# Spreading the last projections over twelve heads, and mixing tile 0 one head later

## The reference, cut to what matters

```python
proj = einsum('bsd,de->bse', rmsnorm(x), w_in)      # a_u a_v a_z b_q b_k b_v b_z i_q i_k i_w
ya = spatial_gating(a_u, a_v, ...)                  # branch A
yb = sparse_attention(q, k, b_v, qi, ki, wi)        # branch B: 8 heads, 256 keys of each row
oa, ob = rmsnorm(ya per group), rmsnorm(yb per head)
mixed = concat([oa * silu(a_z), ob * silu(b_z)])
x = x + einsum('bse,ed->bsd', mixed, w_out)
```

## Time and profile before

| | |
|---|---|
| runs | 601.02, 600.10, 600.96 us; median 600.96 us |
| span of the profiled execution, first to last instruction | 597.3 us |
| PE busy | 561.4 us (94%) |
| DVE busy | 448.7 us (75%) |
| ACT busy | 375.5 us (63%) |
| POOL busy | 229.4 us (38%) |
| mean granted PE clock | 0.983 of full |

### The profile page before, as it was taken

One profiled execution on the slowest core, in us unless ns is written; L12 is line 12 of the kernel. 1 busy time (PEld: TensorE's weight loads), 2 busy tenths in 40 slices (PEclk: granted clock), 3 DMA queues, 4 the chain that ended last, 5 costly groups with the idle time before them and its releaser, 6 DMA issues.

```text
span 597.3 us, 9151 instructions
## 1 busy us (share of the span) xinstructions
PE 561.4 (94%) x3038; PEld 477.2 (80%) x3038; DVE 448.7 (75%) x1142; ACT 375.5 (63%) x743; POOL 229.4 (38%) x300
## 2 busy tenths in 40 slices
PE   8798999989999999979999997999989899999987
PEld 7796888868878888868878786888878788898866
DVE  4574788889999887778999557788777877657631
ACT  6573767757898885757877645655455455555510
POOL 5686432118865456675333425731011010102020
PEclk9899999989999999999999997899999999999999
DMA  8622210012321112212112337012201102020122
GB/s 238 223 72 62 63 36 18 2 36 73 105 88 38 53 37 54 71 36 54 35 54 88 98 120 224 0 54 72 81 26 49 58 10 62 19 72 2 36 71 70
DMA packets 39982, 39.69 MB, mean 66 GB/s; under 512 B 6144, under 2 KB 28160, under 8 KB 39936
## 3 DMA queue, kind: packets, MB, share of 16 engines
q1 hardware_dynamic: 38896, 39.11, 22.1%
q10 hardware_dynamic: 1040, 0.00, 0.1%
HBM read 30.72 MB, written 8.39 MB: 65 GB/s over the span
## 4 chain that ended last, share of the span: by engine, by line
PE 52%; DVE 25%; POOL 10%; issue 6%; ACT 4%; DMA 2%; DVEq 0%; SPq 0%; POOLq 0%; ACTq 0%
PE ps_proj L1071 15%; PE ps_proj L1237 11%; PE ps_proj L1207 5%; PE ps_lg L1099 4%; PE ps_lg L1098 4%; PE ps_tp L1192 4%; DVE y_a L1577 3%; DVE rank L1456 2%; POOL w_lo L620 2%; PE ps_lg L1237 2%; DVE eq L1456 2%; DVE cand L1467 2%; DVE delta L1472 2%; POOL stage L615 2%; POOL y_a L682 1%
## 5 line engine op out<-in xcount | busy, mean ns | idle before, releaser
L1071 PE MATMUL ps_proj<-w_hi,xT_hi 128*128 128x512 f32 (+1 forms) x432 | 166.4, 385 | 5.6 <-POOL w_lo L620 4.3
L1071 PE MATMUL ps_proj<-w_lo,xT_hi 128*128 128x512 f32 (+1 forms) x432 | 162.5, 376 | 0.0
L1071 PE MATMUL ps_proj<-w_hi,xT_lo 128*128 128x512 f32 (+1 forms) x432 | 162.4, 376 | 0.0
L908 ACT ACTIVATE ps_lg<-score,cand 128x768 f32<-128x768 f32 (+2 forms) x96 | 96.2, 1002 | 27.5 <-DVE cand L1467 27.5
L620 POOL TENSOR_TENSOR w_lo<-stage,w_hi 128x512 fp32r<-128x512 f32 x48 | 64.5, 1344 | 97.1 <-ACT w_hi L769 97.1
L1071 PEld LDWEIGHTS ps_proj<-w_hi,xT_hi 128*128 128x128 f32 x432 | 82.8, 192 | 19.9 <-POOL w_lo L620 5.6
L1071 PEld LDWEIGHTS ps_proj<-w_lo,xT_hi 128*128 128x128 f32 x432 | 82.5, 191 | 15.1
L1071 PEld LDWEIGHTS ps_proj<-w_hi,xT_lo 128*128 128x128 f32 x432 | 83.0, 192 | 12.4
L973 ACT CAST xT_hi<-ps_tp 128x512 fp32r<-128x512 f32 (+3 forms) x96 | 43.9, 483 | 63.8 <-PE ps_tp L1192 63.5
L1699 DVE TENSOR_TENSOR xT_lo<-ps_tp,xT_hi 128x512 fp32r<-128x512 f32 (+3 forms) x96 | 50.8, 553 | 33.7 <-ACT xT_hi L973 33.3
L732 POOL TENSOR_TENSOR yz<-hi_f,lo_f 128x512 f32<-128x512 f32 x8 | 10.3, 1285 | 124.7 <-DVE hi_f L1716 124.0
(11 more groups left out here) (176 smaller groups left out, 1169.2 us busy)
## 6 DMA issues: line engine op xcount, KB each, us to landing
stage<-in_w_in_dram SPq DMA_DIRECT2D x48, 256.0 KB, 2.6
x_in<-in_x_dram SPq DMA_DIRECT2D x8, 512.0 KB, 6.0
lo_f<-in_x_dram SPq DMA_DIRECT2D x7, 512.0 KB, 4.0
out_dram<-lo_f SPq DMA_DIRECT2D x7, 512.0 KB, 3.5
q_scratch<-nat SPq DMA_DIRECT2D x8, 256.0 KB, 2.1
q_in<-q_scratch SPq DMA_DIRECT2D x8, 256.0 KB, 3.3
stage<-in_w_out_dram SPq DMA_DIRECT2D x8, 256.0 KB, 2.7
z_scratch<-nat SPq DMA_DIRECT2D x8, 256.0 KB, 2.0
```

The costliest lines, as they stand in the source:

```text
L908: act.activation(ps_lg[i % 2][:, 0:keys(t)], score[:, sc_off[t]:sc_off[t] + keys(t)], ACT.Sign, bias=cand[:, t:t + 1].bitcast(F32), scale= ...
L1071: mm = pe.matmul(ps_proj[u % 2][:, 0:n], a[:, k, rows], b[:, k, 0:n], start=(k == 0 and i == 0), stop=(k == KB - 1 and i == 2))
```

## The change

The 32 blocks are allotted 2, 2, 2, 2 to heads 0 to 3 and 3 each to heads 4 to 11, where they were 3 each for heads 0 to 9 and 2 for head 10. Everything that is worked out from the list moves with it: units 4 to 7 are now completed in heads 3, 6, 9 and 11 (tanh, gate, store and the cast of a w_out block go with them), and `W_FROM` is 12. And DVE's `mix_b(0)` stands at the end of head 13 in place of head 12; the later tiles' stay where they were.

```diff
-        STEPS_BZ = [3] * 10 + [2]
+        STEPS_BZ = [2] * 4 + [3] * 8
...
                     if h == 2 and t > 0:
                         y_sums(t - 1)
-                    if h == 4 and t > 0:
+                    if h == (5 if t == 1 else 4) and t > 0:
                         mix_b(t - 1)
```

## The result

The changed kernel takes 603.95 us (median of 20 runs, 601.16 to 606.86), the kernel before 600.14 us (20 runs, 597.21 to 603.29): ratio 1.0059, 95% interval 1.0044 to 1.0073. It is slower by 0.6%: 3.5 us by the ratio, 3.8 by the two medians. That is outside the range of the prediction (600.0 to 603.2), on the side that it held a little less likely than no change.

A forecast was written before the change was run, and what follows sets the result against it. Between 362.7 and 377.2 the chain from unit 7 to the mix, not PE's speed, was taken to set the end. Terms of -0.04 up to 377.15 and +1.3 for the clock, on 600.96, gave 602.2 us; range 600.0 to 603.2.

The forecast's parts named there:

- W_out's second half: Casts, splits and scales of w_out's second half come a head later, first needed in head 17, hidden: costed at nothing.
- Heads 0 to 10 and unit 7: Head 0 saves nothing, the 0.22 us wait goes, head 10 ends about 1.65 us earlier; unit 7 complete 1.37 us later.
- Heads 11 to 13: Head 11's 2.67 us wait is filled; PE waits some 1.85 us for `lo_pT(11)`, replacing both old waits.
- The chain to the mix: From unit 7, durations stay: store 2.92 us, factors 1.37 us later, `mix_b(0)` 1.67 us, ending at 374.46.
- rival B: Chain from unit 7: store lands in 2.0 us or `mix_b` takes 0.7; time 600.3, down to 600.0; chance 0.12.
- The place of the mix: `mix_b(0)` in head 13 lets `mT(0, 0)` run at about 369.2, before the wait; first output block 377.15 against 377.19.
- The clock: After a wait of nearly 5 us PE stays at 1.2 GHz until 380.0, losing 1.3 us from the first output block.
- Rival C: Heads 11 to 13 at full clock: less low clock is itself a gain, 1.8 us, time 599.2; chance 0.08.

The follow-up runs named there:

- the two freed runs: Changed kernel with tile 0's mixing on POOL freed of unit 7: 597.57 us (0.9948); also with tile 1's mixing before the last split: 597.78 us (0.9938).

## Why the prediction was wrong

**The step that failed** is "W_out's second half": "Casts, splits and scales come a head later. They are first needed in head 17 ... I cost these at nothing." It asked when PE needs the blocks, and that part is right: no profile shows PE waiting for a block of this half in heads 17 to 22. It did not ask what stands behind the last split on POOL. `finish_b(1)` does, and DVE needs it in head 20. The price of the late casts, by the marks, is 24.1 - 21.6 = 2.5 us where the prediction had nothing: 1.5 for `finish_b(1)` behind the last split, 1.0 for POOL's scale and split falling beside DVE's steps. By the medians the casts alone cost 1.9 us, and taking tile 1's mixing out of that place, or the casts back, removed some 2.8 of the change's 3.5 us. All rivals of the prediction lay before head 15; none had this mechanism.

**Heads 0 to 10 and unit 7** were right. Head 0 saved nothing (a wait of 0.53), the 0.22 us wait went, and unit 7 was complete at 363.34 (its blocks in the chain start at 361.27 and take 2.07), which is 363.86 with the 0.52 added, where 364.04 was worked out.

**Heads 11 to 13** were right: 1.72 us before `pv(5)`, where 1.85 was worked out; `mT(0, 0)` at 368.55 + 0.52 = 369.07, worked out 369.2.

**The chain to the mix** was right in kind, and a little long. The mix began at 371.48 and took 1.66 us, so `mT(0, 1)` ran at 373.19 + 0.52 = 373.71, worked out 374.55. In this execution the store was not the last thing that `yz` waited for:

```profile
367.78 1.28 POOL L732 TENSOR_TENSOR yz<-hi_f,lo_f 128x512 f32<-128x512 f32 x1
```

It has no wait at all: POOL was itself busy till then, with the split and two scales, and the gap of 0.73 us that lay there before was not needed. In this execution rival B all but came true up to head 15: `mT(0, 1)` before 373.8, the first output block at 376.55, where it had 376.4 or earlier. The second profile of the changed kernel (the change again; first scores at 332.20, so 0.64 us is to be taken off) goes as forecast. Its `yz` waits for the store, and `mT(0, 1)` comes at 374.85 - 0.64 = 374.21 after a wait of 4.51:

```profile
369.43 1.28 POOL L732 TENSOR_TENSOR yz<-hi_f,lo_f 128x512 f32<-128x512 f32 x1 [0.47 <-DMA z_scratch<-nat]
...
374.85 1.12 PE L1230 MATMUL ps_tp<-ident,hi_f 128*128 128x128 f32 x4 [4.51 <-DVE hi_f L1724]
```

Its first output block is at 377.68 - 0.64 = 377.04, worked out 377.15. The loss of the change stands behind this point in both. (One reading of the prediction was wrong without effect: not all of PE's waits in rows 3 end with DVE; the one of 2.67 us ends with ACT.)

**The place of the mix** was right in mechanism, as the run without the move shows (4.72 and 6.16 us of waiting), with 0.7 us in the medians, not beyond doubt.

**The clock.** Forecast was 1.2 GHz till 380.0, a loss of 1.3 us. The profiled execution had full clock back at about 376.4; the second one of the same kernel, entered 1.16 us later, at about 379.8 (PE: stretch and its length, busy, granted clock, DMA):

```profile
376.00:376.50 0.50, 0.50 (x3) 0.56 0.00 0
```

```profile
379.50:380.00 0.50, 0.50 (x3) 0.71 0.00 0
```

From the first output block to the return of the clock are 0.4 and 2.1 us. At the prediction's own rate that is a loss of 0.2 us in the first and 1.0 in the second, whose middle stretch is 24.9 in place of 24.1. So the term varies from one execution to the next, and 1.3 was above both. What nearness the forecast time has to the measured one, 602.2 to 603.95, is luck: a loss that was smaller than forecast stood for one that I had not seen, and the sum started from the 600.96 us of three runs, where twenty gave 600.14.

**Rival C,** that less low clock is a gain as such, fell for the change: the first profile of the changed kernel has 3.4 us of low clock from head 14 on and as much behind head 22, against 10.2 before, and its span is 2.9 us longer. By the penalty in the Trainium skill ("TensorE: Matmul & The Clock Gate", section "Terms") it would have been the faster (an estimate: half of the 3.4 us less, 1.7 us). The rival's condition, `mT(0, 1)` not waiting long for the mix, was nearly made by the two freed runs with spread blocks and late casts (a wait of 1.6 us, no low clock in this stretch), and there the 2.7 and 3.5 us under the kernel before were gained. Whether the low clock or the waits themselves were the price, these runs don't part.

**What stays open.** With the casts back, or tile 1's mixing first, 0.7 and 0.8 us over the kernel before remain, with intervals that just hold no change. In the first case the marks show ACT's wait in head 12 (46.5 against 45.6). In the second the two small waits of 0.41 and 0.38 us are still there, with 1.2 GHz beyond the first output block; which of them makes the rest isn't shown. Open too is what tile 1's mixing behind the split costs: 1.5 us by the marks, some 2.8 by the medians where it was moved in the changed kernel, and at most 0.6 (by the ratios, within their intervals) between the two freed runs that part in it.

## What to carry to other kernels

When a step is moved by a slot, walk down every queue that it is in, to the next consumer of whatever stands behind it. The split that came a head later was in time for its own reader, with heads to spare, but the mixing queued behind it was late for DVE. And a gain that is swallowed by a chain isn't lost: the spreading measured 0.0% alone and 0.5% once POOL's two mixings were out of its way and the casts begun in head 12, so a neutral or losing change is worth one profile of what it waits for before it is dropped.

## What the runs showed of the hardware

**A DVE product and a POOL split take turns.** The mix of tile 0 took 1.66 us in the changed kernel, as before, with POOL's split starting 0.15 us ahead of it. In the run with only the casts late, no split was ready, the mix began first and took 0.69 us, and it was the split that became longer, 1.72 us in place of 1.27. DVE, then POOL, of that run:

```profile
370.41 0.69 DVE L1724 TENSOR_TENSOR hi_f<-yz,yr 128x512 f32<-128x512 f32 x1 [0.21 <-POOL yr L741]
...
370.51 1.72 POOL L620 TENSOR_TENSOR w_lo<-hi_f,w_hi 128x512 fp32r<-128x512 f32 x1 [0.21 <-ACT w_hi L767]
```

The Trainium skill ("SBUF — State Buffer", section "SBUF: two separate sides") says that the port pair shared by the two goes to the one that starts first, for its whole instruction, when DVE reads two SBUF tensors and the GpSimd instruction reads SBUF; these rows agree, with 1.0 us for the one that comes second on DVE and 0.45 on POOL. By these rows, 1.0 of the edit's 1.1 us in the first column of the marks can be this; no run has it by itself.

**One kernel's executions spread by 1%, and the clock goes with it.** With only the casts late, the fastest of twelve took 599.70 us at a mean granted clock of 0.988 and the slowest 606.93 at 0.972.
